# Hybrid attention and recurrence layer: the attention gate as a third unit of the dense stage, and a reordered attention loop

## What is computed

```
proj = h @ w_in
aq, ak, av, ag, rq, rf, ri, rg = split(proj)      # widths 1024, 256, 256, 1024, 4 x 1024
aq, ak = rope(rms_norm(aq)), rope(rms_norm(ak))   # 16 query heads, 4 key heads, 64 wide
attn = sliding_window_attention(aq, ak, av, sinks) * silu(ag)    # window 128
rec  = rms_norm(hgrn2_chunkwise(rq, f(rf), ri)) * silu(rg)       # 8 heads of 128, chunks of 64
out  = x + gate * (concat(attn, rec) @ w_out)
```

## Time and profile before

| | us |
|---|---|
| median of three runs (lowest, highest) | 2014.29 (2012.52, 2015.05) |
| the profiled execution: its time, its span | 2012.31, 2010.5 |
| TensorE matmul busy | 1912.3 |
| TensorE weight load busy (beside the matmuls) | 1621.2 |
| VectorE busy | 1061.9 |
| ScalarE busy | 876.6 |
| GpSimd busy | 529.1 |
| TensorE's mean granted clock, as a share of full | 0.981 |

### The profile page before, as it was taken

How to read it: one execution, slowest core, us unless ns; L and a number is a source line. 1 busy time by engine, 2 the same in 40 slices (tenths; PEclk the granted TensorE clock), 3 DMA queues, 4 the chain that set the end, 5 groups by cost and what they waited for, 6 DMA issues and landing times. The chain is left out here.

```text
span 2010.5 us, 31984 instructions
## 1 busy us (share of the span) xinstructions
PE 1912.3 (95%) x11436; PEld 1621.2 (81%) x11436; DVE 1061.9 (53%) x2476; ACT 876.6 (44%) x2041; POOL 529.1 (26%) x865
## 2 busy tenths in 40 slices
PE   5999999999969999899999999997999979999999
PEld 3888989898858888678898988885888868888887
DVE  6956554545527665695745454555755562222212
ACT  3523455655636555542346555554565461101100
POOL 1002454445413333200244454441333210000000
PEclk9999999999979999899999999998999989999999
DMA  9143201011023342433320111104232172222221
GB/s 345 54 147 124 80 12 70 14 65 58 11 94 107 117 149 86 147 110 126 116 83 18 67 40 43 52 13 168 69 111 75 52 257 96 92 94 94 83 83 42
DMA packets 145034, 184.12 MB, mean 92 GB/s; under 512 B 8992, under 2 KB 117920, under 8 KB 138784
## 3 DMA queue, kind: packets, MB, share of 16 engines
q1 hardware_dynamic: 144928, 182.73, 26.9%
HBM read 133.82 MB, written 48.89 MB: 91 GB/s over the span
## 5 line engine op out<-in xcount | busy, mean ns | idle before, releaser
L707 PE MATMUL bank<-h_hi,w_hi 128*128 128x256 f32 (+1 forms) x1024 | 361.4, 353 | 13.2 <-ACT k_f L1250 10.0
L707 PE MATMUL bank<-h_hi,w_lo 128*128 128x256 f32 (+1 forms) x1024 | 347.2, 339 | 0.0
L707 PE MATMUL bank<-h_lo,w_hi 128*128 128x256 f32 (+1 forms) x1024 | 346.9, 339 | 0.0
L707 PEld LDWEIGHTS bank<-h_hi,w_hi 128*128 128x128 f32 x1024 | 196.2, 192 | 60.3 <-issue 22.8
L707 PEld LDWEIGHTS bank<-h_lo,w_hi 128*128 128x128 f32 x1024 | 195.9, 191 | 21.7
L707 PEld LDWEIGHTS bank<-h_hi,w_lo 128*128 128x128 f32 x1024 | 196.4, 192 | 19.2 <-issue 0.5
L707 PE MATMUL bank<-wo_hi,m_hi 128*128 128x512 f32 x512 | 203.1, 397 | 5.9 <-DVE m_lo L1826 5.9
L707 PE MATMUL bank<-wo_hi,m_lo 128*128 128x512 f32 x512 | 200.3, 391 | 0.0
L707 PE MATMUL bank<-wo_lo,m_hi 128*128 128x512 f32 x512 | 199.9, 391 | 0.0
L1171 ACT ACTIVATE sm<-sm,neg_m 128x256 f32<-128x256 f32 x256 | 127.3, 500 | 139.3 <-DVE sink_d L1611 139.3
L707 PE MATMUL bank<-w_hi,h_hi 128*128 128x384 f32 x512 | 177.3, 346 | 3.5 <-DVE qn L1649 1.7
(11 more groups left out here) (216 smaller groups left out, 4218.9 us busy)
## 6 DMA issues: line engine op xcount, KB each, us to landing
raw<-in_w_in SPq DMA_DIRECT2D x24, 1024.0 KB, 8.3
g_raw<-in_w_in SPq DMA_DIRECT2D x16, 1024.0 KB, 6.6
nat_rows<-u SPq DMA_DIRECT2D x48, 256.0 KB, 2.6
raw<-in_w_in SPq DMA_DIRECT2D x8, 1536.0 KB, 6.1
wa<-in_w_ada SPq DMA_DIRECT2D x8, 1024.0 KB, 11.7
mixed_cols<-o_mix SPq DMA_DIRECT2D x64, 128.0 KB, 1.8
r_v<-nat_rows SPq DMA_DIRECT2D x32, 256.0 KB, 2.9
rg_w<-nat_rows SPq DMA_DIRECT2D x32, 256.0 KB, 2.9
```

The source lines that it names most:

```text
L707: mm = pe.matmul(dst, a, b, start=(first and m == 0), stop=(last and m == 2), **more)
```

## The change

The gate's columns ag leave the attention loop. They become unit 1 of GU = 3 in the dense stage. In this unit the weights are the stationary side and the tokens the moving one, so the result comes out with features on the partitions; `block_out` writes it to a new DRAM array gate_T. The attention loop reads it back, 128 KB for each block and group, into g_q, four blocks ahead; ScalarE takes its tanh (g_t) and VectorE multiplies.

The attention loop is written out for all 32 blocks of a segment. The projections go to banks 0 and 1 in turn, so that a projection needs the bank of the block before last. LAG is 4. TensorE's order in a round becomes: projection b, transposes of q and k of b-1, transposes of p of b-3, p times v of b-4, scores of b-1. ScalarE: exponentials b-2, square b, copies of v, q, k, copy of pT b-3, normalization b-2, tanh b-3, then in rounds 2 and 5 of every eight one half of the next group's high weights. VectorE: masks b-2, gate product b-4, denominator b-2, row sum b, low parts b-1, copy of pT b-3, qn b, o_mix b-4, then in rounds 2 and 5 one half of the low weights. The weights of q, k, v have two homes, wq_hi and wq_lo 0 and 1. In the last group the two halves are those of recurrence head 0; head 1 is split at step 1 of the recurrence. GpSimd's list is the same.

```diff
-ATT_UNIT, REC_UNIT = REG[0] + REG[1], KT * 2 * RK
-LAG = 3
-GU = 2
+REG = KT * QKV
+REC_UNIT = KT * 2 * RK
+LAG = 4
+GU = 3
+GATE_U = 1
+ATT_B = GROUPS * NBLK
 GQ = KH * HALF
...
+        wq_hi = [place(AT_S + i * 2 * REG * 4, f"wq_hi{i}", [P, REG], F32R) for i in range(2)]
+        wq_lo = [place(AT_S + (i * 2 + 1) * REG * 4, f"wq_lo{i}", [P, REG], F32R) for i in range(2)]
...
+            def block_out(s, u, tile, done, t_half, n_half, c):
+                if u == GATE_U:
+                    t0 = s * SEG + t_half * QUAD
+                    sp.dma_start(gate_Tf[:, n_half * 4 + c, t0:t0 + QUAD], tile[:]).then_inc(done, 16)
+                else:
...
+                def load_next(g):
+                    sp.wait_ge(lo_ok[0], 2 * w_use(s, 0, g) + 2)
+                    if g + 1 < GROUPS:
+                        load_att(g + 1)
+                    else:
+                        load_rec(0)
...
+                for b in range(4):
+                    load_gate_block(b)
+                load_next(0)
+                load_rec(1)
+                for b in range(ATT_B):
+                    g, i = b // NBLK, b % NBLK
+                    att_spill(b)
+                    if b + 4 < ATT_B:
+                        load_gate_block(b + 4)
+                    if i == 2 and s > 0 and g + 1 < GROUPS:
+                        carried(g + 1)
+                    if i == 3 and g + 1 < GROUPS:
+                        load_next(g + 1)
...
                 for k in range(KH):
-                    ah, al = operand(c, k)
-                    wh, wl = g_hi[N % 2][:, k, :], g_lo[N % 2][:, k, :]
-                    mm = split_products(ring(n, at + c)[:, :], ((ah, wh), (ah, wl), (al, wh)), fresh and k == 0,
-                                        k == KH - 1, skip_group_check=not fresh)
+                    ah, al = operand(k)
+                    wh, wl = g_hi[w_slot(n, e)][:, k, :], g_lo[w_slot(n, e)][:, k, :]
+                    if n % GU == GATE_U:
+                        wh, wl = wh[:, tokens(c)], wl[:, tokens(c)]
+                        pairs = ((wh, ah), (wl, ah), (wh, al))
+                    else:
+                        ah, al = ah[:, tokens(c)], al[:, tokens(c)]
+                        pairs = ((ah, wh), (ah, wl), (al, wh))
+                    mm = split_products(ring(n, at + c)[:, :], pairs, fresh and k == 0, k == KH - 1,
+                                        skip_group_check=not fresh)
                 mm.then_inc(blk_ok, 1)
 
...
+            def att_iter(s, b):
+                S = s * ATT_B
+                if b < ATT_B:
+                    g, i = b // NBLK, b % NBLK
+                    if b == NBLK // 2:
                         pe.wait_ge(hop_ok, (PRODS + 1) * (s + 1))
-                    if past >= 1:
-                        pe.wait_ge(qn_ok, n + i)
-                        pe.wait_ge(v_read, n + i)
-                    project(0, w, i == 0, lambda k: project_rows(bank[0][:, 0:QKV], 0, i, 0, QKV, QKV, k)
+                    if b >= 2:
+                        pe.wait_ge(qn_ok, S + b - 1)
+                        pe.wait_ge(v_read, S + b - 1)
+                    project(0, w_use(s, 0, g), i == 0, lambda k: project_rows(bank[b % 2][:, 0:QKV], g, i, k)
                             ).then_inc(qkv_ok, 1)
...
+                if 1 <= b <= ATT_B:
+                    j = b - 1
+                    pe.wait_ge(rot_ok, S + j + 1)
+                    if j >= 1:
...
+                if 3 <= b <= ATT_B + 2:
+                    j = b - 3
+                    pe.wait_ge(pn_ok, S + j + 1)
+                    if j >= 1:
+                        pe.wait_ge(pta_ok, S + j)
...
+                if 4 <= b <= ATT_B + 3:
+                    j = b - 4
+                    pe.wait_ge(pta_ok, S + j + 1)
+                    pe.wait_ge(ptv_ok, S + j + 1)
+                    if j >= 1:
+                        pe.wait_ge(omix_ok, S + j)
...
+                if 1 <= b <= ATT_B:
+                    j = b - 1
+                    pe.wait_ge(tcopy_ok, 2 * (S + j + 1))
+                    if j >= 1:
+                        pe.wait_ge(masked_ok, GH * (S + j))
...
+                if 3 <= b <= ATT_B + 2:
+                    j = b - 3
+                    act.wait_ge(pt_ok, S + j + 1)
+                    if j >= 2:
+                        act.wait_ge(pv_ok, S + j - 1)
+                    act.activation(pT[j % 2][:, 0:2, :, :].rearrange("p h a q -> p (h a q)"), bank[5][:, :],
+                                   ACT.Copy).then_inc(pta_ok, 1)
...
+                if 3 <= b <= ATT_B + 2:
+                    j = b - 3
+                    act.wait_ge(gq_in[j % 4], 16 * ((S + j) // 4 + 1))
+                    if j >= 2:
+                        act.wait_ge(gs_ok, S + j - 1)
+                    act.activation(g_t[j % 2][:], g_q[j % 4][:], ACT.Tanh, scale=0.5).then_inc(gth_ok, 1)
+                if b < ATT_B and b % NBLK in (2, 5):
+                    g, half = b // NBLK, (2, 5).index(b % NBLK)
+                    if g + 1 < GROUPS:
+                        act.wait_ge(raw_in[0], 16 * w_use(s, 0, g + 1) + 16)
+                        att_weights_hi(g + 1, half)
+                    else:
+                        rec_weights_hi(s, 0, (half,))
 
...
+            def att_weights_lo(s, g, half):
+                at = slice(half * (REG // 2), (half + 1) * (REG // 2))
+                dve.wait_ge(hi_ok[0], 2 * w_use(s, 0, g) + half + 1)
+                dve.tensor_tensor(wq_lo[g % 2][:, at], raw[0][:, at], wq_hi[g % 2][:, at].bitcast(F32), ALU.subtract
+                                  ).then_inc(lo_ok[0], 1)
+
+            def rec_weights_lo(s, h, halves=(0, 1)):
+                r, use = unit_of(h)
+                for half in halves:
+                    at = slice(half * (REC_UNIT // 2), (half + 1) * (REC_UNIT // 2))
+                    dve.wait_ge(hi_ok[r], 2 * w_use(s, r, use) + half + 1)
+                    dve.tensor_tensor(w_lo[r][:, at], raw[r][:, at], w_hi[r][:, at].bitcast(F32), ALU.subtract
+                                      ).then_inc(lo_ok[r], 1)
 
...
+                if 4 <= b <= ATT_B + 3:
+                    j = b - 4
+                    dve.wait_ge(gth_ok, S + j + 1)
+                    dve.scalar_tensor_tensor(g_q[j % 4][:], g_t[j % 2][:], 1.0, g_q[j % 4][:], ALU.add, ALU.mult
+                                             ).then_inc(gs_ok, 1)
...
+                if 3 <= b <= ATT_B + 2:
+                    j = b - 3
+                    dve.wait_ge(pt_ok, S + j + 1)
+                    if j >= 2:
+                        dve.wait_ge(pv_ok, S + j - 1)
+                    dve.tensor_copy(pT[j % 2][:, 2:4, :, :].rearrange("p h a q -> p (h a q)"),
+                                    bank[6][:, :]).then_inc(ptv_ok, 1)
+                if b < ATT_B:
...
+                if 4 <= b <= ATT_B + 3:
+                    j = b - 4
+                    dve.wait_ge(pv_ok, S + j + 1)
+                    dve.wait_ge(gs_ok, S + j + 1)
+                    if j >= 2:
+                        dve.wait_ge(att_out[j % 2], 16 * ((S + j) // 2))
+                    for t in range(2):
+                        a = dve.scalar_tensor_tensor(o_mix[j % 2][:, t, :], bank[7][:, t * P:(t + 1) * P], 0.5,
+                                                     g_q[j % 4][:, t, :], ALU.mult, ALU.mult)
+                    a.then_inc(omix_ok, 1)
+                if b < ATT_B and b % NBLK in (2, 5):
+                    g, half = b // NBLK, (2, 5).index(b % NBLK)
+                    if g + 1 < GROUPS:
+                        att_weights_lo(s, g + 1, half)
+                    else:
+                        rec_weights_lo(s, 0, (half,))
 
             def normalize_half(m):
...
+        if u == GATE_U:
+            halves = [((COL_G, HALF),), ((COL_G + HALF, HALF),)]
```

More of the change, by code:

```diff
@@ L163, in hybrid_layer @@
         wa_sum = [wa_sum0, wa_sum1]
[L165 to L170, removed]
@@ L178, in hybrid_layer @@
[L178 to L181, removed]
+        wide, small = [P, GH + 1, HD], [P, 8]
+        sizes = [("kT_hi", [P, NBLK + 1, P], F32R), ("kT_lo", [P, NBLK + 1, P], F32R)]
+        sizes += [(f"pT{i}", [P, GH, 2, P], F32) for i in range(2)]
+        sizes += [("vv", [P, NBLK + 1, HD], F32), ("row_max", small, F32), ("den2", small, F32)]
@@ new lines, in hybrid_layer, with at_slot @@
+        sizes += [(f"{n}{i}", small, F32) for n in ("neg_m", "sink_d", "den", "sink_e", "r_den") for i in range(2)]
+        named = {}
+        def at_slot(at, limit, sizes):
+            made, end = row(AT_W + at, *sizes)
+            assert end <= AT_W + limit
+            named.update(zip([n for n, _, _ in sizes], made))
+        at_slot(0, 20480, sizes)
+        at_slot(20480, 24576, [("sq", wide, F32), ("qn", wide, F32), ("rc", wide, F32)])
+        at_slot(24576, 32768, [(f"sm{i}", [P, GH, 2 * P], F32) for i in range(2)])
@@ new lines, in hybrid_layer @@
```

(30 more changed lines are left out.)

520 lines of the change are left out of this document (194 added, 326 removed).

## The result

| | before | after |
|---|---|---|
| median of six runs each, us | 2012.85 (2011.92 to 2015.05) | 2021.7 (2019.85 to 2026.43) |
| the profiled execution: its time, its span | 2012.31, 2010.5 | 2026.43, 2024.6 |
| VectorE busy | 1061.9 | 1128.7 |
| mean granted clock | 0.981 | 0.970 |

The change makes the kernel slower: ratio 1.0046, 95% interval 1.0032 to 1.0059, some 9 us.

What follows compares the result with a forecast made beforehand. TensorE was taken to bound attention. Dense and attention -7.5, tails -2, recurrence +2 and clock +8.5 make +1 on 2012.3, so 2013.3; the median's 2.0 offset gives 2015.3 us, range 1972 to 2046.

Steps and rivals of the forecast that it cites:

- attention, the clock in it: Attention to its last scores: 268.2 us per segment instead of 348.15, with +8.5 in all for the clock.
- recurrences: Head 1's split, moved into the recurrence's second step, mostly hides behind projections: +2 us in all, between 0 and 5.
- The unit: Dense stage: the gate as one more unit costs 76.2 us per segment, 152.4 for both; stationary weights cost nothing.
- The round: Attention: TensorE's round falls from 10.53 to 7.46 us, level with the 7.44 us loop from square to square.
- the rival that it is longer: Attention: sink_d held behind q_rot makes the square-to-square loop exceed TensorE's round by about 0.7 us; 2056, or 2035; chance 0.15.
- The splits: Attention: splitting the next weights makes masks 3.5 us late; TensorE loses 3.1 us each, 2.3 for recurrence head 0.
- The clock: Attention: half clock after waits before the scores, taken for half of 12 splits at 1.4 us: +8.5, bounds 0 and 27.
- The prediction's rival, that the clock falls behind every split: Attention: recurring waits set TensorE back to 1.2 GHz after every split, 27 us instead of 8.5: 2034; chance 0.10.
- The fill: Attention's first blocks: scores end at 13.8, near 20.9 and, with the first split, near 30.3 us.
- The tails: After attention's last scores: same steps in another order, -2 us for both tails, with 5 either way.
- Transfers: Gate store and reads: 64 more reads of 128 KB, wanted over 22 us later, cost nothing.

Runs made afterwards that it cites:

- e0: The changed kernel with the twelve splits inside attention only 8 columns wide, other head groups' weights left out; 1982.27 us, ratio 0.9838.
- e7: The changed kernel with quartered splits, head 1 split in attention's last round, and unread matmuls keeping TensorE busy in the loop's fill; 1959.46 us, ratio 0.9736.
- e3: The changed kernel with splits in quarters: high in rounds 2 to 5, low in rounds 4 to 7 behind the gate's product; 1965.32 us, ratio 0.9759.
- e1: The changed kernel with VectorE's low half of each split one round later, at the same place in its round; 1994.8 us, ratio 0.9905.
- e5: The changed kernel with recurrence head 1's split moved from the recurrence's step 1 into attention's last round; 2022.37 us, ratio 1.0044.
- e2: The changed kernel with VectorE's low half one round later and in its idle stretch behind the gate's product; 1972.71 us, ratio 0.9797.

## Why the prediction was right, and where it was off

The forecast was 2015.3, slower with the greatest chance, in a range of 1972 to 2046. The median came at 2021.7, in the forecast's own range of 2003 to 2030. By its steps, for both segments together, on the profiled executions:

| | predicted | measured |
|---|---|---|
| dense stages, with the gate's unit | +152.4 | +155.2 (76.3 and 78.9) |
| attention, the clock in it | -159.9 + 8.5 = -151.4 | -69.0 - 68.2 = -137.2 |
| tails | -2 | -7.3 |
| recurrences | +2 | +4.0 |
| sum, with the start and the output stage | +1 | +14.1 |

*The unit.* 231.48 us for the dense stage was predicted as 231: the pitch of the earlier trace rows held with the weights on the stationary side. In segment 1 it cost 2.7 more.

*The round.* Predicted 7.46 from the earlier trace rows, measured 7.49, and no wait in an ordinary round. The loop from square to square is level, as said, and the rival that it is longer did not come true. What I had not priced is how thin its ground is: 0.15 us between sink_d and q_rot (e0).

*The splits.* The order of events was right in each step: ScalarE's high half from 334.50 to 335.98, 1.6 us of VectorE's wait released by it, masks 3.4 us late (3.5 predicted). The transposes were held up by 0.3 to 0.5 us (up to 1 predicted). TensorE's loss was 2.8 us a split instead of 3.1, and 2.0 instead of 2.3 for most of those of recurrence head 0. Of this term 4 us were given too much. (Five splits at 3.1 are 15.5, not the 15.7 of the sum; this changes nothing.)

*The clock.* This is the step that failed in size: "half of 12 attention splits at 1.4", +8.5. Not six but ten of those twelve fell, and one of head 0's four, which the term had left out; at 1.5 us each on average this is 16.7. Two waits had given the rate of one in two, and two are few. The prediction's rival, that the clock falls behind every split, was nearer than my half: it fell in 11 of 16 cases, not in each. The prediction cites for it the Trainium skill, TensorE: Matmul & The Clock Gate, section "HAM oscillation — how this bites in real kernels". What that section describes are DMA waits of 3 to 5 us; the waits here are 1.7 to 2.5, so the trace agrees that recurring waits can set the clock back, and shows it for shorter ones.

*The fill.* The second sum that was too short: the third block's scores were to end 30.3 us after the first projection. They ended 34.2 and 33.3 after it. In segment 0 TensorE idled ahead of the first transposes and scores and then ran at about half clock into the third projection, which took 6.0 us instead of 4.27:

```profile
293.52 0.44 PE L849 MATMUL bank<-ident,q_rot 128*128 128x128 f32 x2 [2.27 <-POOL q_rot L1949]
...
295.56 0.58 PE L890 MATMUL bank<-kT_hi,qT_hi 64*128 64x256 f32 x2 [1.30 <-DVE kT_lo L1643]
...
297.14 0.69 PE L724 MATMUL bank<-wq_hi,h_hi 128*128 128x384 f32 x1
...
315.24 0.58 PE L890 MATMUL bank<-kT_hi,qT_hi 64*128 64x256 f32 x2 [2.54 <-DVE kT_lo L1643]
```

The sum had no clock in the fill at all; e7 takes 4.4 us of this away in both segments. These two terms, 8.2 and 6.9, with 1.5 for the rounds and less the 4 of the splits, are 12.6 of the 14.2 us missed in attention. Most of the rest is the clock again: five of the rounds with a wait are longer than the others of their kind, 1.4 us together, since their scores ran slowly already (10.64 against 10.31 us).

*The tails* gave 5.0 and 2.3 us instead of 1 each; the first of them ran at a mean clock of 0.99 against 0.74 in the earlier trace rows. That made up for part of the miss, by luck: the prediction took 1 us each from the order of the work and had no term for the clock there. Luck has a second share. On the profiled executions 14.1 us were measured for the predicted 1; the median is only 6.4 us above the forecast because the profiled execution of after is the slowest of its six.

*Transfers.* No tanh waited for one: 64 reads of 128 KB landed in 2.4 us (median). In the attention stages the store and load of the gate cost nothing visible.

Against before, then: with the splits in quarters elsewhere (e3), the change is worth 47 us. As it was made, the waits behind the splits took 42 of them back, because the splits stand where the masks queue behind them, and the clock 15 more, which leaves it some 9 us slower. Of TensorE's work alone 44 us were to be saved; 64 rounds of 7.49 instead of 10.53 us, less the 155.2 of the dense stages, are 39.

## What to carry to other kernels

When a loop has been shortened until two engines are level, look for every operation that is not in each round, and follow what queues behind it; cut it up and put it where its engine waits anyway. Price a recurring stall twice: its own length, and the work behind it at half clock, which here followed most idle times of about 2 us. A trial with work for TensorE in the wait tells the two apart.

## What the runs showed of the hardware

*Idle time and the clock.* Ahead of the scores, in after: behind 10 waits of 1.85 to 2.06 us 8 projections ran at about half clock, behind 4 of 1.72 us one, behind 2 of 2.53 and 2.54 us both. In e1, behind 14 of 1.52 us, none. e5 has the same 16 waits: 11 slow projections again, but in part behind other waits, two of the four of 1.72 us among them and 7 of the 10 of 1.84 to 2.06. e0 has the four of 1.72 us alone, with two slow projections behind them, and behind its ten of 0.69 to 0.84 us none. Together: 0 of 14 at 1.52 us, 5 of 12 at 1.72, 15 of 20 at 1.84 to 2.06, 4 of 4 at 2.53 or 2.54. So length sets a chance and not the outcome; the runs do not show why two of equal length (344.22 and 478.40) differ.

*VectorE against GpSimd.* A subtraction of 128x1536 from SBUF took 1.76 us where GpSimd's product beside it was held to its end (0.47 to 1.99), and 2.12 and 2.29 in the middle of that list (e1, e2), while GpSimd's product went from 0.46 to 1.97. A 128x4 operation of 0.16 us took 0.74 (e1). This agrees with the rule of the Trainium skill, SBUF — State Buffer, section "SBUF: two separate sides", that such a pair excludes each other for a whole instruction. New to me was its effect at small size: an operation on four columns can be the costly one, and a delay of 0.64 us became 0.76.
